# A hybrid encoder trunk in Bass: four sums of W2 quarters made by accumulating DMAs instead of GpSimd subtractions

## The chip, the cores and the metric

The kernel runs on one core of a Trainium2 chip. The metric is the device time of one execution in microseconds (us); lower is better. Engines are called by the names of the profile: PE (TensorE), PEld (its weight loads), DVE (VectorE), ACT (ScalarE), POOL (GpSimd) and SP (SyncE, which only issues DMAs here).

## The reference, cut to what matters

Two layers over 512 tokens of width 1024 in float32. Layer 0 mixes tokens by differential attention, layer 1 by a pooling mixer. Each layer then adds an MLP with a hidden width of 4096:

```
def sqrelu_mlp(h, w1, w2):
    return jnp.square(jax.nn.relu(h @ w1)) @ w2
...
h = rmsnorm(x, norm_mlp[i])
x = x + sqrelu_mlp(h, mlp_w1[i], mlp_w2[i]).astype(x.dtype)
```

The change touches only `u @ w2`, where `u` is the squared hidden activation.

## The kernel before

**Stages.** The attention layer's work fills the span up to about 310 us; then come the MLP of layer 0, the pooling mixer (about 650 to 720 us) and the MLP of layer 1. Every float32 matmul is made of three: a value is split into a part `_hi` (an ACT copy with rounding to fp32r) and a rest `_lo` (a DVE subtraction of two SBUF tensors), and PE computes hi*hi, hi*lo and lo*hi (`three`).

**MLP blocks.** The hidden width is cut into 8 blocks of 512 for each layer: b = 0 to 7 in layer 0 and 8 to 15 in layer 1. `up(b)` is 96 matmuls (`h @ w1`), then `products(b)` is 84 matmuls (`u @ w2` of the block). The last block of a layer (7 and 15, `plain`) multiplies in the ordinary way. The other 14 use a Strassen-Winograd scheme: u and W2 are each cut into four quarters, and seven products take the place of eight. For this, W2's quarters B11, B12, B21 and B22 (512 KB each) are loaded by SP, and four combinations are formed from them by POOL in `w2_sum`:

```
T1 = B12 - B11    T3 = B22 - B12 (written over B12)
T2 = B22 - T1     T4 = T2 - B21
```

The four combinations of u (S3, S1, S2, S4) are formed by DVE in `part_sum`. The products run in the order P1, P7, P6, P5, P2, P3, P4 and need B11, T3, T2, T1, B21, B22 and T4 in this order; each has 12 matmuls.

**What sets the order.** Each engine runs a written-out list and waits on semaphores. For POOL: T1, T3, T2, T4 of block b as soon as the products of block b-1 have freed T1's buffer (P5) and T4's (P4) and the quarters have landed; in blocks 1 to 4, `band(b-1)` (small masks for the pooling mixer) follows. For ACT in `up_phase(b)`: the hi part of T3, a piece of the next block's W1, the hi part of T2, another piece of W1, then the squares of the hidden tiles. For DVE in `up_phase(b)`: two lo parts of W1 (`w1_lo(b, 2)`, `(b, 3)`), lo of B11, T3, T1, one of W1, lo of T2, one of W1, and then `hidden(b, 0)`, the first look at up's output. The lo part of a matrix is written over its raw buffer, so DVE's `w2_low` for T1 also waits until T2 (which reads T1) is made, and that for T2 waits until T4 is made. In `down_phase(b)` DVE alternates lo parts with `gather`, which adds each finished product into an accumulator and frees its PSUM bank; P4 needs the lo part of T4 and the bank that P5's gather frees. Near the end of the layer `sums` combines the seven accumulators.

In block 0, POOL makes T1 between `norm_sums(0)` and `norm_root(0)`, and T3, T2, T4 after `norm_root(0)`. In block 8 it makes all four between `norm_root(1)` and `norm_sums(2)`, in the pooling stage. SP's list places `load_w2(b+1)` between the two halves of a W1 load; the load of a quarter waits for the product that last read its buffer (`PIECE_FREED`).

Of the kernel before, what the change touches and what calls it, by code (L numbers as in the profile page):

```python
# [144 lines left out]
HI_HOME = {B11: 0, B21: 0, T3: 1, B22: 1, T2: 2, T4: 2, T1: 3}  # L145
PLAIN_HOME = {B11: 0, B12: 1, B21: 2, B22: 3}
PIECES = (B11, B12, B21, B22)
PIECE_FREED = {B11: P1, B12: P7, B21: P2, B22: P3}
T_ORDER = (T1, T3, T2, T4)
U_ORDER = (A11, S3, S2, S1, A12, S4, A22)  # L150
S_ORDER = (S3, S1, S2, S4)

# [9 lines left out]
def first(b):  # L162
    return b % NB == 0
# [6 lines left out]
def before_block(b, each, last):  # L170

    layer, j = divmod(b, NB)
    return layer * ((NB - 1) * each + last) + j * each


def y_at(b):
    return before_block(b, 2 * NP, NU)
# [11 lines left out]
    return before_block(b, len(S_ORDER), 0)  # L189


def t_at(b):
    return before_block(b, len(T_ORDER), 0)


def build_trunk(nc, x, positions, norm_mix, norm_mlp, w_qkv, w_o, q_gain, k_gain, lam_q1, lam_k1,
                lam_q2, lam_k2, sub_gain, pool_w, pool_scale, w1, w2, out):
    ctx = ExitStack()
    with ctx:
# [29 lines left out]
        def sem(name):  # L229
            return ctx.enter_context(nc.semaphore(name))  # L230
# [161 lines left out]
        y_ready = sem("y_ready")  # L392
        y_added = sem("y_added")
        w2_loaded = {n: sem(f"w2_loaded_{n}") for n in PIECES}
        t_done = sem("t_done")
        w2_hi_done = sem("w2_hi_done")
        w2_lo_done = sem("w2_lo_done")
        up_piece = sem("up_piece")
# [88 lines left out]
        @block.sync  # L487
        def _(sp):
            xv = x.rearrange("a (t p) d -> p (a t) d", p=P)
            for t in range(NT):  # L490
                sp.dma_start(x_nat[:, t, :], xv[:, t, :]).then_inc(x_loaded[t], 16)
                sp.dma_start(raw[t][:].rearrange("p (a b) -> p a b", a=2), piece(0, t)).then_inc(raw_loaded[t], 16)

            def load(slab, k, src, width=PIECE):

                sp.wait_ge(w_lo_done, slab * 4 + (k - 3))
                dst = raw[k][:, 0:width]
                if len(src.shape) == 3:
                    dst = dst.rearrange("p (a b) -> p a b", a=src.shape[1])
                sp.dma_start(dst, src).then_inc(raw_loaded[k], 16)  # L500

            for s in range(1, MLP0):
                for k in range(4):
                    load(s, k, piece(s, k))

            wait_used(sp, WO0 - 1)
            for t in range(NT):
                sp.dma_start(x_again[:, t, :], xv[:, t, :]).then_inc(x_again_loaded[t], 16)

            def load_w1(b, ks):  # L510
                for k in ks:
                    load(w1_slab(b), k, w1_piece(b, k))

            def load_pool(ks):
                for k in ks:
                    load(POOLS, k, piece(POOLS, k), 2 * GW)

            def load_w2(b):
                for n in PIECES:
                    if b == 0:  # L520
                        sp.wait_ge(wo_ready, 2 * NC)
                    elif first(b):
                        sp.wait_ge(y_ready, y_at(b))
                    else:
                        sp.wait_ge(y_ready, y_at(b - 1) + 2 * PIECE_FREED[n] + 2)
                    sp.dma_start(w2_raw[n][:], w2_piece(b, n)).then_inc(w2_loaded[n], 16)

            load_w1(0, range(4))
            load_w1(1, range(4))
            load_w2(0)  # L530
            for b in range(2 * NB - 1):
                if b == NB - 2:
                    load_pool((0, 1))
                    load_w2(b + 1)
# [12 lines left out]

            ov = out.rearrange("a (t p) d -> p (a t) d", p=P)
            for n, (t, nh) in enumerate(UNITS):
                sp.wait_ge(y_added, y_at(2 * NB - 1) + n + 1)  # L550
                sp.dma_start(ov[:, t, nh * BANK:(nh + 1) * BANK], sum_part((t, nh))).then_inc(stored[n % 4], 16)
            for k in range(4):
                sp.wait_ge(stored[k], 16 * (NU // 4))
# [3 lines left out]
        def _(pool):  # L557
# [174 lines left out]

            def w2_sum(b, n):

                if n == T1:
                    pool.wait_ge(w2_loaded[B11], 16 * (b + 1))
                    pool.wait_ge(w2_loaded[B12], 16 * (b + 1))
                    if not first(b):
                        pool.wait_ge(y_ready, y_at(b - 1) + 2 * P5 + 2)
                    one, two = B12, B11  # L740
                elif n == T3:
                    pool.wait_ge(w2_loaded[B22], 16 * (b + 1))
                    pool.wait_ge(t_done, t_at(b) + 1)
                    one, two = B22, B12
                elif n == T2:
                    one, two = B22, T1
                else:
                    pool.wait_ge(w2_loaded[B21], 16 * (b + 1))
                    pool.wait_ge(t_done, t_at(b) + 3)
                    if not first(b):  # L750
                        pool.wait_ge(y_ready, y_at(b - 1) + 2 * P4 + 2)
                    one, two = T2, B21
                g.tensor_tensor(w2_raw[n][:], w2_raw[one][:], w2_raw[two][:], ALU.subtract).then_inc(t_done, 1)  # L753

            def band(gi):
                w = WINDOWS[gi]
# [49 lines left out]
        def _(act):  # L806
# [24 lines left out]
            def w2_hi(b, n):  # L831

                if n in PIECES:
                    act.wait_ge(w2_loaded[n], 16 * (b + 1))
                else:
                    act.wait_ge(t_done, t_at(b) + T_ORDER.index(n) + 1)
                if plain(b):
                    home = PLAIN_HOME[n]
                    act.wait_ge(y_ready, y_at(b - 1) + 2 * (P2, P3, P4, P5)[home] + 2)
                else:  # L840
                    home = HI_HOME[n]
                    if n in (B21, B22, T4):
                        act.wait_ge(y_ready, y_at(b) + 2 * (P1, P7, P6)[home] + 2)
                    elif not first(b):
                        act.wait_ge(y_ready, y_at(b - 1) + 2 * (P2, P3, P4, P5)[home] + 2)
                a.activation(b_hi[home][:], w2_raw[n][:], ACT.Copy).then_inc(w2_hi_done, 1)  # L846
# [241 lines left out]
        def _(dve):  # L1088
# [39 lines left out]
            def w2_low(b, n):  # L1128

                if plain(b):  # L1130
                    home, order = PLAIN_HOME[n], PLAIN_ORDER
                else:
                    home, order = HI_HOME[n], W2_ORDER
                    if n != T3:
                        dve.wait_ge(t_done, t_at(b) + {B11: 1, T1: 3, T2: 4, B21: 4, B22: 3, T4: 4}[n])
                dve.wait_ge(w2_hi_done, w2_at(b) + order.index(n) + 1)
                v.tensor_tensor(w2_lo[n][:], w2_raw[n][:], f32(b_hi[home][:]), ALU.subtract).then_inc(w2_lo_done, 1)  # L1137

# [188 lines left out]
            def part_sum(b, n):  # L1327

                done = s_at(b) + S_ORDER.index(n)
                if n == S3:  # L1330
                    dve.wait_ge(u_done, CH * b + 2)
                    one, two, op = A11, "A21", ALU.subtract
                elif n == S1:
                    dve.wait_ge(u_done, CH * b + CH)
                    one, two, op = "A21", A22, ALU.add
                elif n == S2:
                    dve.wait_ge(s_done, done)
                    one, two, op = S1, A11, ALU.subtract
                else:
                    dve.wait_ge(s_done, done)  # L1340
                    one, two, op = A12, S2, ALU.subtract
                v.tensor_tensor(u_part[n], u_part[one], u_part[two], op).then_inc(s_done, 1)  # L1342

            def part_lo(b, n):
                dve.wait_ge(u_hi_done, u_at(b) + U_ORDER.index(n) + 1)
# [77 lines left out]

            def sums(b):

                def combine_sums(dst, one, two, op=ALU.add):
                    return v.tensor_tensor(acc[dst][:], acc[one][:], acc[two][:], op)

                dve.wait_ge(y_added, y_at(b))
                link(combine_sums(P2, P1, P2))  # L1430
                link(combine_sums(P6, P1, P6))
                link(combine_sums(P7, P6, P7))
                yield
                link(combine_sums(P4, P7, P4, ALU.subtract))
# [567 lines left out]
```

## Time and profile before

| | |
|---|---|
| median of 3 runs | 1052.71 us (1051.85 to 1053.17) |
| the profiled execution, its own time | 1052.46 us |
| its span, first to last instruction | 1050.7 us |
| busy share of the span | PE 94%, PEld 76%, DVE 83%, ACT 46%, POOL 41% |
| mean granted TensorE clock | 0.985 |
| read and written | 92.74 MB, mean 88 GB/s |

A busy time is the sum of an engine's recorded instructions. Matmuls are pipelined and their records overlap, so PE's stalls are read from the distances between the starts of its matmuls, not from its share. All loads of W2 quarters are one group of 64 DMAs of 512 KB each.

### The profile page before, as it was taken

What the parts mean: (1) busy time and instruction counts of PE and PEld (TensorE: products, weight loads), DVE (VectorE), ACT (ScalarE), POOL (GpSimd) and SP (SyncE); (2) the same over time, 40 slices, a digit from 0 to 9 for tenths busy, and PEclk for the clock granted to TensorE, in tenths of its full rate; (3) what the DMA queues carried; (4) which work ended last, traced back from release to release, by engine and by line L of the source; (5) the groups of instructions that cost most, each with busy time, mean ns of one, the idle gap of its engine ahead of it and who ended that gap; (6) DMA issues with size and microseconds to landing.
All of it is one profiled execution on the core that took longest, in us unless ns stands there. A gap on an engine that the chain in (4) does not pass through costs nothing.

```text
span 1050.7 us, 12852 instructions
## 1 busy us (share of the span) xinstructions
PE 989.1 (94%) x4676; PEld 802.4 (76%) x4676; DVE 874.3 (83%) x1125; ACT 479.6 (46%) x735; POOL 429.0 (41%) x377
## 2 busy tenths in 40 slices
PE   6999998889899799999999999798999999999998
PEld 5877776667677588887887887696887888788887
DVE  5667889877946999999998897676988989989884
ACT  4525555677644534425435353364452442543420
POOL 5852678556447173473840300371403304124000
PEclk9999999999999999999999999989999999999999
DMA  6423211120232333332333233301323333233102
GB/s 240 146 42 100 61 41 58 63 81 1 62 99 80 100 100 102 99 106 95 108 93 107 74 106 115 120 2 42 119 87 113 100 101 103 98 100 100 61 20 80
DMA packets 52046, 92.74 MB, mean 88 GB/s; under 512 B 8848, under 2 KB 9872, under 8 KB 51984
## 3 DMA queue, kind: packets, MB, share of 16 engines
q1 hardware_dynamic: 45888, 91.24, 27.4%
q10 hardware_dynamic: 6096, 0.69, 0.5%
q8 instruction: 37, 0.61, 0.2%
q14 instruction: 25, 0.20, 0.1%
HBM read 89.82 MB, written 2.10 MB: 87 GB/s over the span
## 4 chain that ended last, share of the span: by engine, by line
PE 53%; DVE 27%; issue 8%; POOL 5%; ACT 4%; DMA 1%; ACTq 1%; DVEq 0%; SPq 0%; POOLq 0%
PE bank L1572 51%; DVE s_s_raw L1342 3%; DVE s_acc L1360 3%; DVE s_lbB_lo L1137 3%; ACT s_u_raw L994 2%; DVE s_w_lo L1117 2%; DVE s_nmax L1227 2%; DVE s_u_raw L1324 2%; POOL s_nsum L727 2%; PE bank L1630 1%; DVE s_u_lo L1348 1%; DVE s_lt_lo L1137 1%; DVE s_p L1249 1%; DVE s_a_lo L1348 1%; POOL s_o_r L702 1%
## 5 line engine op out<-in xcount | busy, mean ns | idle before, releaser
L1572 PE MATMUL bank<-s_hT_hi,s_w_hi 128*128 128x512 f32 x512 | 200.5, 392 | 0.0
L1572 PE MATMUL bank<-s_hT_hi,s_w_lo 128*128 128x512 f32 x512 | 199.4, 389 | 0.0
L1572 PE MATMUL bank<-s_hT_lo,s_w_hi 128*128 128x512 f32 x512 | 199.4, 389 | 0.0
L1117 DVE TENSOR_TENSOR s_w_lo<-s_raw,s_w_hi 128x1024 fp32r<-128x1024 f32 x96 | 165.9, 1744 | 14.3 <-ACT s_w_hi L816 7.9
L1572 PE MATMUL bank<-s_b_hi,s_u_hi 128*128 128x512 f32 x288 | 117.1, 407 | 14.2 <-DVE s_a_lo L1348 10.4
L753 POOL TENSOR_TENSOR s_lt<-s_lbB,s_lbB 128x1024 f32<-128x1024 f32 x14 | 35.0, 2498 | 222.9 <-PE bank L1572 222.9
L846 ACT ACTIVATE s_b_hi<-s_lbB 128x1024 fp32r<-128x1024 f32 x64 | 67.3, 1054 | 128.2 <-POOL s_lbB L753 84.5
L1572 PEld LDWEIGHTS bank<-s_hT_lo,s_w_hi 128*128 128x128 f32 x512 | 96.2, 188 | 20.2 <-issue 0.5
L1572 PEld LDWEIGHTS bank<-s_hT_hi,s_w_hi 128*128 128x128 f32 x512 | 96.2, 188 | 20.2 <-issue 0.5
L1572 PEld LDWEIGHTS bank<-s_hT_hi,s_w_lo 128*128 128x128 f32 x512 | 96.1, 188 | 20.0
L1360 DVE TENSOR_TENSOR s_acc<-s_acc,bank 128x512 f32<-128x512 f32 x168 | 107.5, 677 | 2.0 <-PE bank L1572 2.0
L1137 DVE TENSOR_TENSOR s_lbB_lo<-s_lbB,s_b_hi 128x1024 fp32r<-128x1024 f32 x64 | 104.2, 1652 | 0.0
L994 ACT ACTIVATE s_u_raw<-s_u_raw 128x512 f32<-128x512 f32 x64 | 39.9, 632 | 121.2 <-DVE s_u_raw L1324 121.1
L824 ACT ACTIVATE s_w_hi<-s_raw 128x1024 fp32r<-128x1024 f32 x60 | 61.6, 1051 | 71.2 <-PE bank L1572 63.1
L1572 PE MATMUL bank<-s_lbB_lo,s_u_hi 128*128 128x512 f32 x232 | 91.5, 394 | 0.0
L1572 PE MATMUL bank<-s_w_hi,s_hT_hi 128*128 128x512 f32 x192 | 80.1, 417 | 8.4 <-DVE s_val L1191 3.8
L1572 PE MATMUL bank<-s_b_hi,s_s_lo 128*128 128x512 f32 x224 | 87.2, 389 | 0.0
L1572 PEld LDWEIGHTS bank<-s_b_hi,s_u_hi 128*128 128x128 f32 x288 | 54.8, 190 | 35.5 <-issue 20.8
L1572 PE MATMUL bank<-s_w_hi,s_hT_lo 128*128 128x512 f32 x192 | 77.1, 402 | 0.0
L1572 PE MATMUL bank<-s_w_lo,s_hT_hi 128*128 128x512 f32 x192 | 76.9, 401 | 0.0
L1572 PE MATMUL bank<-s_b_hi,s_u_lo 128*128 128x512 f32 x176 | 68.8, 391 | 0.0
L1572 PE MATMUL bank<-s_b_hi,s_s_hi 128*128 128x512 f32 x168 | 65.5, 390 | 1.0 <-DVE s_s_lo L1348 1.0
(195 smaller groups left out, 2186.8 us busy)
## 6 DMA issues: line engine op xcount, KB each, us to landing
s_raw<-in_mlp_w SPq DMA_DIRECT2D x64, 512.0 KB, 3.8
s_lbB<-in_mlp_w SPq DMA_DIRECT2D x64, 512.0 KB, 3.3
s_raw<-in_attn_w_qkv SPq DMA_DIRECT2D x24, 512.0 KB, 4.2
s_raw<-in_attn_w_o SPq DMA_DIRECT2D x8, 512.0 KB, 3.4
s_x_nat<-in_x SPq DMA_DIRECT2D x4, 512.0 KB, 8.5
s_x_again<-in_x SPq DMA_DIRECT2D x4, 512.0 KB, 5.2
out<-s_acc SPq DMA_DIRECT2D x8, 256.0 KB, 2.0
s_raw<-in_pool_w SPq DMA_DIRECT2D x4, 256.0 KB, 2.6
```

Source lines behind the costliest of these rows:

```text
L727: g.tensor_tensor(nsum[:], first_sum, nsq[:, c % 2, :], ALU.add).then_inc(n_summed, 1)
L753: g.tensor_tensor(w2_raw[n][:], w2_raw[one][:], w2_raw[two][:], ALU.subtract).then_inc(t_done, 1)
L824: a.activation(w_hi[0][:, k * PIECE:(k + 1) * PIECE], raw[k][:], ACT.Copy).then_inc(w_hi_done, 1)
L846: a.activation(b_hi[home][:], w2_raw[n][:], ACT.Copy).then_inc(w2_hi_done, 1)
L994: a.activation(u_raw[:, f, :], u_raw[:, f, :], ACT.Square).then_inc(u_done, 1)
L1117: v.tensor_tensor(w_lo[slot][:, cols], raw[k][:], f32(w_hi[slot][:, cols]), ALU.subtract)\
L1137: v.tensor_tensor(w2_lo[n][:], w2_raw[n][:], f32(b_hi[home][:]), ALU.subtract).then_inc(w2_lo_done, 1)
L1227: last = v.tensor_reduce(nmax[:, i % 2, m:m + 1], bank[2 * (i % 2) + m][:], AX.X, ALU.max, negate=True)
L1324: v.scalar_tensor_tensor(u_raw[:, f, :], up_bank(b, f)[:], 0.0, r_bc[:], ALU.max, ALU.mult)\
L1342: v.tensor_tensor(u_part[n], u_part[one], u_part[two], op).then_inc(s_done, 1)
L1360: last = v.tensor_tensor(dst, dst, src, ALU.add)
L1572: return nc.tensor.matmul(o, lhsT, rhs, start=start, stop=stop, **kw)
```

## The change

POOL's four subtractions in each of the 14 blocks become four DMAs that POOL issues (`g.dma_start(..., accum_op=ALU.add)`): the DMA reads its source, adds it to what its destination holds, and writes the sum there. Since these DMAs only add, all combinations become sums (T1 = B11 + B12, T3 = B12 + B22, T2 = B22 + T1, T4 = B21 + T2). The signs are moved into the combinations of the activations (`part_sum`) and of the accumulators (`sums`); two instructions in each block and two in `sums` become `scalar_tensor_tensor`, where one operand is negated.

An accumulating DMA needs one term in its destination first. So SP also loads B11 into T1's buffer, B22 into T2's and B21 into T4's: seven loads in a block instead of four. T1 and T3 add a quarter straight from HBM; T2 and T4 add T1 and T2 from SBUF. SP's loads wait for the products in the order in which these free the buffers (`FREED_BY`). Each T has its own semaphore. The lo part of B11, B21, B22 and T4 no longer waits for a T; that of T1 still waits for T2 and that of T2 for T4.

```
-PIECE_FREED = {B11: P1, B12: P7, B21: P2, B22: P3}
+FREED_BY = {B11: P1, B12: P7, T2: P6, T1: P5, B21: P2, B22: P3, T4: P4}
+LOAD_ORDER = tuple(FREED_BY)
+T_PARTS = {T1: (B11, B12), T3: (B12, B22), T2: (B22, T1), T4: (B21, T2)}
...
+def sums_to(b):
+    return before_block(b, 1, 0) + 1
...
             def load_w2(b):
-                for n in PIECES:
+                for n in PIECES if plain(b) else LOAD_ORDER:
...
-                        sp.wait_ge(y_ready, y_at(b - 1) + 2 * PIECE_FREED[n] + 2)
-                    sp.dma_start(w2_raw[n][:], w2_piece(b, n)).then_inc(w2_loaded[n], 16)
+                        sp.wait_ge(y_ready, y_at(b - 1) + 2 * FREED_BY[n] + 2)
+                    if n in PIECES:
+                        sp.dma_start(w2_raw[n][:], w2_piece(b, n)).then_inc(w2_loaded[n], 16)
+                    else:
+                        sp.dma_start(w2_raw[n][:], w2_piece(b, T_PARTS[n][0])).then_inc(t_loaded[n], 16)
...
             def w2_sum(b, n):
...
-                g.tensor_tensor(w2_raw[n][:], w2_raw[one][:], w2_raw[two][:], ALU.subtract).then_inc(t_done, 1)
+                if n == T3:
+                    pool.wait_ge(w2_loaded[B12], 16 * (b + 1))
+                else:
+                    pool.wait_ge(t_loaded[n], 16 * sums_to(b))
+                two = T_PARTS[n][1]
+                if two in PIECES:
+                    src = w2_piece(b, two)
+                else:
+                    pool.wait_ge(t_done[two], 16 * sums_to(b))
+                    src = w2_raw[two][:]
+                g.dma_start(w2_raw[n][:], src, accum_op=ALU.add).then_inc(t_done[n], 16)
...
-                    if n != T3:
-                        dve.wait_ge(t_done, t_at(b) + {B11: 1, T1: 3, T2: 4, B21: 4, B22: 3, T4: 4}[n])
+                    if n in (T1, T2):
+                        dve.wait_ge(t_done[T2 if n == T1 else T4], 16 * sums_to(b))
...
-                v.tensor_tensor(u_part[n], u_part[one], u_part[two], op).then_inc(s_done, 1)
+                if n in (S1, S3):
+                    last = v.tensor_tensor(u_part[n], u_part[one], u_part[two], ALU.subtract)
+                else:
+                    last = v.scalar_tensor_tensor(u_part[n], u_part[one], -1.0, u_part[two], ALU.mult, ALU.subtract)
+                last.then_inc(s_done, 1)
```

## Rows read from the trace of the kernel before

**Rows 1.** The page, busy time and share of the span of each engine.

```profile
PE 989.1 (94%) x4676; PEld 802.4 (76%) x4676; DVE 874.3 (83%) x1125; ACT 479.6 (46%) x735; POOL 429.0 (41%) x377
```

**Rows 2.** Windows, products of block 2: PE, PEld, DVE, ACT, POOL, clock, DMA share, GB/s.

```profile
434.04:453.58 19.54, 19.39 (x84) 15.77 (x85) 19.27 (x27) 10.82 (x14) 2.39 (x1) 1.00 0.33 108
```

**Rows 3.** Timeline of PE, block 2: start us, us, then [idle before].

```profile
434.04 0.47 PE L1572 MATMUL bank<-s_b_hi,s_u_hi 128*128 128x512 f32 x1 [0.43 <-DVE s_a_lo L1348]
...
450.24 0.39 PE L1572 MATMUL bank<-s_b_hi,s_s_lo 128*128 128x512 f32 x1
450.77 0.47 PE L1572 MATMUL bank<-s_b_hi,s_u_hi 128*128 128x512 f32 x1
...
453.58 0.39 PE L1572 MATMUL bank<-s_hT_hi,s_w_hi 128*128 128x512 f32 x1
```

**Rows 4.** Timeline of DVE, end of block 2 and start of block 3.

```profile
445.72 2.58 DVE L1348 TENSOR_TENSOR s_u_lo<-s_u_raw,s_u_hi 128x512 fp32r<-128x512 f32 x1
...
454.73 6.02 DVE L1117 TENSOR_TENSOR s_w_lo<-s_raw,s_w_hi 128x1024 fp32r<-128x1024 f32 x2
...
469.66 1.21 DVE L1117 TENSOR_TENSOR s_w_lo<-s_raw,s_w_hi 128x1024 fp32r<-128x1024 f32 x1
471.46 0.69 DVE L1324 SCALAR_TENSOR_TENSOR s_u_raw<-bank,s_r_bc 128x512 f32<-128x512 f32 x1 [0.59 <-PE bank L1572]
```

**Rows 5.** Timeline of POOL, the sums T1 and T3 for block 3.

```profile
445.36 2.39 POOL L753 TENSOR_TENSOR s_lt<-s_lbB,s_lbB 128x1024 f32<-128x1024 f32 x1 [11.86 <-PE bank L1572]
453.94 2.40 POOL L753 TENSOR_TENSOR s_lbB<-s_lbB,s_lbB 128x1024 f32<-128x1024 f32 x1 [6.20 <-DMA s_lbB<-in_mlp_w]
```

**Rows 6.** The tile s_u_lo on DVE, blocks 1 and 14: ns min/median/max, first and last start.

```profile
L1348 DVE TENSOR_TENSOR s_u_lo<-s_u_raw,s_u_hi x2: 687/1652/2617, 399.7 to 403.8; 128x512 fp32r<-128x512 f32 x2
...
L1348 DVE TENSOR_TENSOR s_u_lo<-s_u_raw,s_u_hi x2: 683/684/685, 988.4 to 992.5; 128x512 fp32r<-128x512 f32 x2
```

**Rows 7.** Timeline of PE before P4, blocks 0 and 13.

```profile
366.34 0.39 PE L1572 MATMUL bank<-s_b_hi,s_s_lo 128*128 128x512 f32 x1
367.17 0.47 PE L1572 MATMUL bank<-s_b_hi,s_u_hi 128*128 128x512 f32 x1 [0.45 <-DVE s_acc L1357]
...
955.38 0.39 PE L1572 MATMUL bank<-s_b_hi,s_s_lo 128*128 128x512 f32 x1
955.91 0.47 PE L1572 MATMUL bank<-s_b_hi,s_u_hi 128*128 128x512 f32 x1
```

**Rows 8.** W2 loads (L526): all 64, then first and last of four issued together.

```profile
DMA to landing us min/median/max: 3.1/3.3/7.4
...
L526 SPq DMA_DIRECT2D s_lbB<-in_mlp_w x1: 368/368/368, 318.0 to 318.0; - x1
DMA to landing us min/median/max: 3.5/3.5/3.5
...
L526 SPq DMA_DIRECT2D s_lbB<-in_mlp_w x1: 467/467/467, 319.4 to 319.4; - x1
DMA to landing us min/median/max: 7.1/7.1/7.1
```

**Rows 9.** Timelines of POOL, DVE and PE, start of block 0.

```profile
334.52 2.38 POOL L753 TENSOR_TENSOR s_lbB<-s_lbB,s_lbB 128x1024 f32<-128x1024 f32 x1
336.86 2.83 POOL L753 TENSOR_TENSOR s_lt<-s_lbB,s_lt 128x1024 f32<-128x1024 f32 x1
...
344.04 1.27 DVE L1324 SCALAR_TENSOR_TENSOR s_u_raw<-bank,s_r_bc 128x512 f32<-128x512 f32 x2
...
347.51 0.77 PE L1572 MATMUL bank<-s_b_hi,s_u_hi 128*128 128x512 f32 x1 [4.78 <-DVE s_a_lo L1348]
```

**Rows 10.** Timelines, pooling stage: POOL's T4 for block 8, DVE and PE beside it.

```profile
692.08 2.40 POOL L753 TENSOR_TENSOR s_lt<-s_lt,s_lbB 128x1024 f32<-128x1024 f32 x1
...
693.16 1.86 DVE L1300 SCALAR_TENSOR_TENSOR s_hT_lo<-s_xT,s_gcol,s_hT_hi 128x512 fp32r<-128x512 f32 x1 [1.52 <-ACT s_hT_hi L979]
...
696.64 0.33 PE L1572 MATMUL bank<-s_band_hi,s_zn_hi 128*128 128x136 f32 x1 [0.69 <-DVE s_zn_lo L1521]
```

More of the change, by code:

```diff
@@ L189, in s_at @@
     return before_block(b, len(S_ORDER), 0)
-def t_at(b):
-    return before_block(b, len(T_ORDER), 0)
+def sums_to(b):
+    return before_block(b, 1, 0) + 1
 def build_trunk(nc, x, positions, norm_mix, norm_mlp, w_qkv, w_o, q_gain, k_gain, lam_q1, lam_k1,
@@ L394, in build_trunk @@
         w2_loaded = {n: sem(f"w2_loaded_{n}") for n in PIECES}
-        t_done = sem("t_done")
+        t_loaded = {n: sem(f"t_loaded_{n}") for n in (T1, T2, T4)}
+        t_done = {n: sem(f"t_done_{n}") for n in T_ORDER}
         w2_hi_done = sem("w2_hi_done")
@@ L733, in w2_sum @@
             def w2_sum(b, n):
-                if n == T1:
-                    pool.wait_ge(w2_loaded[B11], 16 * (b + 1))
+                if n == T3:
                     pool.wait_ge(w2_loaded[B12], 16 * (b + 1))
[L738 to L746, printed above, removed]
-                else:
[L748 to L752, printed above, removed]
-                g.tensor_tensor(w2_raw[n][:], w2_raw[one][:], w2_raw[two][:], ALU.subtract).then_inc(t_done, 1)
+                else:
+                    pool.wait_ge(t_loaded[n], 16 * sums_to(b))
[6 more added lines that the diff above has]
+                g.dma_start(w2_raw[n][:], src, accum_op=ALU.add).then_inc(t_done[n], 16)
             def band(gi):
@@ L835, in w2_hi @@
                 else:
-                    act.wait_ge(t_done, t_at(b) + T_ORDER.index(n) + 1)
+                    act.wait_ge(t_done[n], 16 * sums_to(b))
                 if plain(b):
@@ L1331, in part_sum @@
                     dve.wait_ge(u_done, CH * b + 2)
-                    one, two, op = A11, "A21", ALU.subtract
+                    one, two = A11, "A21"
                 elif n == S1:
                     dve.wait_ge(u_done, CH * b + CH)
-                    one, two, op = "A21", A22, ALU.add
+                    one, two = A22, "A21"
                 elif n == S2:
                     dve.wait_ge(s_done, done)
-                    one, two, op = S1, A11, ALU.subtract
+                    one, two = S1, A11
                 else:
                     dve.wait_ge(s_done, done)
-                    one, two, op = A12, S2, ALU.subtract
-                v.tensor_tensor(u_part[n], u_part[one], u_part[two], op).then_inc(s_done, 1)
+                    one, two = A12, S2
+                if n in (S1, S3):
[3 more added lines that the diff above has]
+                last.then_inc(s_done, 1)
             def part_lo(b, n):
@@ L1424, in sums, with less_sums @@
             def sums(b):
+                def less_sums(dst, one, two):
+                    return v.scalar_tensor_tensor(acc[dst][:], acc[one][:], -1.0, acc[two][:], ALU.mult, ALU.subtract)
                 def combine_sums(dst, one, two, op=ALU.add):
@@ L1433, in sums @@
                 yield
-                link(combine_sums(P4, P7, P4, ALU.subtract))
+                link(combine_sums(P4, P7, P4))
                 yield
-                link(combine_sums(P1, P7, P5))
+                link(less_sums(P1, P7, P5))
                 yield
-                link(combine_sums(P3, P3, P5))
-                link(combine_sums(P3, P3, P6))
+                link(less_sums(P3, P3, P5))
+                link(combine_sums(P3, P3, P6, ALU.subtract))
                 yield
```

## The prediction

> **What bounds the kernel now.** I read the page first, then PE's timeline across one MLP block, then DVE's and POOL's beside it, and last the loads. PE is busy 94% of the span, DVE 83%, POOL 41% [rows 1]. So POOL's time is worth nothing in itself; what counts is what its subtractions do to PE through another engine or a wait.
>
> The products of block 2 run from 434.04 to 453.58, at full clock and with DVE busy 19.27 of 19.54 us [rows 2]. Between 434.04 and 450.24 PE starts 72 matmuls, 0.228 us apart on average [rows 3]. At that pace the block's 180 matmuls take 41.0 us, with the stops below about 41.8. Two places lose time: a stop of 0.43 us before P1, which waits for DVE's a_lo, and one before P4: 450.24 to 450.77 is 0.53 us instead of 0.23, and P4's 12 matmuls then take 2.81 us instead of 2.73 [rows 3]. So P4's stop costs 0.38 us.
>
> P4's stop comes from POOL. At 445.36 it starts T1 of the next block, 2.39 us long [rows 5]. DVE starts the lo part of A22 at 445.72 and is at it for 2.58 us [rows 4]. This instruction takes 0.68 us where nothing is beside it. The lo part of T4 and P5's gather stand behind it in DVE's list, and P4 needs both. The trace has its own control. Each block has two such lo parts (of A12 and A22): in block 1 the longer one took 2617 ns; in block 14, behind which there is no T1 to make, neither took more than 685 ns [rows 6], and PE has no such stop there. A second collision: POOL's T3 at 453.94 [rows 5] and the T2 and T4 that follow lie beside two lo parts of W1 that take 6.02 us together [rows 4], where one alone takes 1.21. It costs nothing now: DVE still waits 0.59 us for PE before `hidden(0)` at 471.46 [rows 4].
>
> **The change part by part, and the sum.**
>
> *The subtractions go* (56 of POOL's instructions). P4's stop goes in blocks 1 to 5 and 9 to 13 (0.38 us, in one of them 0.53), 4.0 us in ten blocks; the last of them is 955.38 to 955.91. In block 0 it is 366.34 to 367.17, 0.83 instead of 0.23, with 0.08 for the restart: 0.7 us [rows 7]. Sum: 4.7 us, from which nothing is taken back as long as no other wait is later than P4. P4 waits for DVE alone here, and DVE comes 2.58 - 0.68 = 1.9 us earlier to a stop of 0.3 us. In the pooling stage T4 of block 8 (692.08) lies beside DVE's lo part at 693.16, 1.86 us instead of 0.75, and PE waits 0.69 us for what comes next on DVE [rows 10]: 0.7 us more. The stops before P1 stay.
>
> *An accumulating DMA: its price.* No row shows one. The nearest is a load of the same 512 KB: 3.3 us from issue to landing, at least 3.1 [rows 8]; that is the lower bound. Four such loads issued within 1.4 us landed 3.5 us after the first issue (321.5) and 7.1 us after the last (326.5) [rows 8]. So three more loads took 5.0 us, 1.7 us each, and this is what one costs the DMA engines; the other 1.6 us are latency. A sum reads its destination as well as its source. I double the 1.7 and keep the latency: 5.0 us. The upper bound is the longest landing in this group, 7.4 us [rows 8]. I take 5.0, since the doubling is the only difference that the change's text shows.
>
> The Trainium skill, "Collectives: The Full Stack", section "The bandwidth ceiling: the fold count and why AG ≠ RS ≠ AR", says that adding in a DMA costs no time of its own, but halves the rate because two sources are read, with 31 GB/s for a DMA engine as its figure for plain copies. No run here shows it yet. By that the moving takes an estimated 2.1 us instead of my 3.4, and a sum about 3.7 us with the same latency.
>
> *The chain of DMAs, steady blocks.* T1's base load can be issued when P5 is done (445.2, as POOL's T1 starts at 445.36 [rows 5]) and lands at 448.5. Then T1, T2 and T4 follow one another, each waiting for the one before: 15 us, 463.5; T3 shares the queue between T1 and T2 and may add up to 1 to 2 us: 465. The deadline: `hidden(0)` starts at 471.46, and the lo parts of T2 and of W1 must come before it, 1.1 us each (469.66 to 471.46 holds the last and the 0.59 of idle time) [rows 4]; so T4 must have landed by 469.2. That leaves 4 to 5 us: hidden, cost 0. The cover is gone when one DMA takes over (469.2 - 448.5)/3 = 6.9 us. Above that, each microsecond costs 3 us in a block, in 12 blocks (1 to 6 and 9 to 14; block 8's are made far ahead).
>
> *More traffic.* A block now moves 8 quarters, 33% of the DMA engines' time [rows 2]. Three more loads and four sums at double price make 19 at 1.7 us, 32 of 41.8 us or 77%. SP's list only gets waits that come in the order of the products, and the W1 loads behind them wait for DVE's lo parts of the following block anyway. Hidden, 0.
>
> *Block 0.* Here nothing covers the sums. POOL makes T3 at 334.52 and T2 until 339.69 [rows 9]; ACT's hi parts and the second W1 lo part follow, `hidden(0)` starts at 344.04 and PE has been idle 4.78 us when P1 starts at 347.51 [rows 9]. Now T3 is issued at 334.5 and lands at 339.5; T2 is right behind it in the queue and lands one service later, 342.9. That is 3.2 us later than 339.7, and it goes straight to PE. As a formula, for a DMA of A us: late by 2A - 6.8 us (issue at 334.5, A for T3, A - 1.6 of service for T2, against 339.7). Bounds: A of 3.3 gives nothing, A of 7.4 gives 8.0 us. I take 3.2. T4 lands at about 348, before DVE reaches the lo part of T2.
>
> *Block 8.* POOL now waits for T1 before it issues T2, and for T2 before T4, with `norm_sums(2)` behind. Counting back three sums of 2.4 us from T4 at 692.08 [rows 10], T1 starts at about 684.8. Two DMAs of 5.0 us later, at 694.8, T4 can be issued, and before, T4 ended at 694.5. Cost 0 up to there, and about 1 us for each further microsecond of a DMA.
>
> *The signs.* Two `scalar_tensor_tensor` in place of `tensor_tensor` in a block, of 512 columns each, and two in `sums` of each layer: DVE's instruction of that kind in the same stage takes 0.69 us [rows 4], about as much. 0.
>
> Sum: -4.7 - 0.7 + 3.2 = -2.2 us. The profiled execution took 1052.46 us, 0.25 below the median of 1052.71, so the forecast for the median is 1050.5 us.
>
> **The rivals.**
>
> *The chain is too slow (slower).* Place: T4's landing against DVE's lo part of T2 in each steady block. It decides from 6.9 us per DMA. At the 7.4 of [rows 8] each of 12 blocks loses 3 x 7.4 - 20.7 = 1.5 us, 18 us, and block 0 loses 8: 1052.7 + 18 + 8 - 5.4 = 1073 us. For it speaks that T3, the bases and the W1 loads share the engines in just these 20 us; against it the 4 us of slack.
>
> *The start of block 0 eats the gain (same).* The steady blocks behave as forecast, but T2 of block 0 lands later. It decides from a DMA of about 5.5 us; at 5.9 it is 2 x 5.9 - 6.8 = 5.0 us late: 1052.7 + 5.0 - 5.4 = 1052.3 us. For it speaks that the doubling is only my estimate.
>
> *The sums are as fast as a load (faster by more).* At the lower bound of 3.3 us T2 of block 0 lands at 339.5 and costs nothing: 1052.7 - 5.4 = 1047.3 us. For it speaks that the load's 1.7 us of service are at the pace of reads from HBM, and T2 and T4 read SBUF alone. By the rate that the Trainium skill's "Collectives: The Full Stack" gives (3.7 us, in the section named above) block 0 would lose an estimated 0.6 us, for 1047.9 us.
>
> *P4's stop stays (slower).* It would if POOL's writing of descriptors held DVE up as the subtraction did: 1052.7 - 0.7 + 3.2 = 1055.2 us, near no change if block 0 loses less. The trace has no DMA issued by POOL, so it can't be excluded.
>
> The Trainium skill, "SBUF — State Buffer", section "Who interferes with whom", says that only two-port modes of DVE block descriptor writing on GpSimd, and that a DVE instruction with two SBUF inputs is held up by GpSimd reading SBUF alone. The 2617 ns of [rows 6] agree with the second half; by the first this rival falls.
>
> **How the numbers follow.** Chances: as forecast 0.30; chain too slow 0.27; sums as fast as a load 0.22; block 0 eats the gain 0.14; P4's stop stays 0.07. The forecast is the likeliest, 1050.5 us, and its own range is 1047.3 to 1053. To hold 8 in 10, the range must take in more than half of the slow chain: up to 1073, its price at 7.4 us. That leaves 0.13 above, and 0.04 below 1047. 0.2% of the time is 2.1 us, about what a measurement of this kernel can tell from no change. The forecast lies at this edge (1050.6), so 0.18 of its 0.30 counts as faster and 0.12 as the same. Faster is 0.18 + 0.22 = 0.40. Same is 0.12, with 0.12 of the eaten gain and 0.02 of the stop that stays: 0.26. Slower is the rest of these two and the slow chain: 0.34.
>
> **What the changed profile would show.** Right: DVE's s_u_lo at 0.68 us in all blocks, PE's starts before P4 0.23 apart, the period from P1 to P1 0.4 us shorter, near 41.4 us, DMAs by POOL landing in 4 to 6 us, and PE's wait before P1 of block 0 grown from 4.8 to about 8 us. Wrong: DVE idle before the lo part of T1 or T2, released by a DMA, `hidden(0)` late in every block, and a period above 42 us; then the chain was too slow. A P4 stop that is still there with short s_u_lo would mean that I named the wrong cause.

## The result, and the profile after

The kernel after takes 1117.6 us (median of 4 runs, 1110.7 to 1121.2) against 1052.9 us for the kernel before beside it. The ratio is 1.059, with an interval of 1.053 to 1.066. That is 65 us slower, 67 above the forecast and 45 above the top of the range.

First, the page of the kernel after: busy time, the DMA queues, the chain of work that ended last, two groups of costly instructions, and DMA issues with their median landing.

```profile
PE 1010.9 (91%) x4676; PEld 820.7 (74%) x4676; DVE 780.7 (70%) x1125; ACT 481.7 (43%) x735; POOL 323.9 (29%) x377
...
q1 hardware_dynamic: 57312, 113.26, 30.6%
q0 software_dynamic: 11648, 29.36, 15.2%
...
PE 39%; DMA 22%; DVE 18%; issue 11%; POOL 6%; ACT 3%; ACTq 0%; POOLq 0%; SPq 0%; DVEq 0%
...
L1578 PE MATMUL bank<-s_b_hi,s_u_hi 128*128 128x512 f32 x288 | 128.0, 444 | 56.9 <-DVE s_a_lo L1351 55.3
...
L1136 DVE TENSOR_TENSOR s_lt_lo<-s_lt,s_b_hi 128x1024 fp32r<-128x1024 f32 x42 | 51.3, 1222 | 46.5 <-DMA s_lt<-s_lt 46.2
...
s_lt<-s_lt POOLq DMA_DIRECT2D x28, 512.0 KB, 7.3
s_lt<-in_mlp_w POOLq DMA_DIRECT2D x14, 512.0 KB, 6.0
s_lbB<-in_mlp_w POOLq DMA_DIRECT2D x14, 512.0 KB, 8.9
```

What the change was to take away is gone: DVE is busy 781 us instead of 874, POOL 324 instead of 429 [rows 1]. In their place stands a chain. A fifth of the time is a DMA that something waits for, DVE waits 46 us for the DMAs of T2 and T4, and PE waits 55 us for `a_lo` before P1.

POOL's timeline in the same stage as [rows 5], the sums for block 3 (start us, us, then the idle time before and what ended it):

```profile
462.93 1.26 POOL L752 DMA_DIRECT2D s_lt<-in_mlp_w  x1 [17.52 <-DMA s_lt<-in_mlp_w]
469.00 1.23 POOL L752 DMA_DIRECT2D s_lbB<-in_mlp_w  x1 [4.81 <-DMA s_lt<-in_mlp_w]
469.73 1.43 POOL L752 DMA_DIRECT2D s_lt<-s_lt  x1
481.67 0.86 POOL L752 DMA_DIRECT2D s_lt<-s_lt  x1 [10.51 <-DMA s_lt<-s_lt]
```

T1 is issued at 462.93, T3 at 469.00, T2 at 469.73, T4 at 481.67. From issue to landing T1 takes 5.8 us, T3 9.0, T2 11.2 (until 481.0) and T4 5.3 (until 487.0); these four together, by the line of the code that issues them:

```profile
DMA to landing us min/median/max: 5.3/7.4/11.2
```

The second line of the timeline is the one to stop at: in the code, T3 waits only for B12's load, issued at 453.73, and yet it goes out when T1 has landed, 6.07 us after T1.

DVE's timeline of the same stage, against [rows 4], and PE's at the stop behind it, before P1 of block 3, to hold against P1 of block 2 in [rows 3]:

```profile
479.16 1.22 DVE L1136 TENSOR_TENSOR s_lbB_lo<-s_lbB,s_b_hi 128x1024 fp32r<-128x1024 f32 x1 [7.73 <-ACT s_b_hi L845]
...
487.01 1.23 DVE L1136 TENSOR_TENSOR s_lt_lo<-s_lt,s_b_hi 128x1024 fp32r<-128x1024 f32 x1 [3.66 <-DMA s_lt<-s_lt]
488.15 1.22 DVE L1116 TENSOR_TENSOR s_w_lo<-s_raw,s_w_hi 128x1024 fp32r<-128x1024 f32 x1
489.29 1.28 DVE L1323 SCALAR_TENSOR_TENSOR s_u_raw<-bank,s_r_bc 128x512 f32<-128x512 f32 x2
```

```profile
488.67 0.39 PE L1578 MATMUL bank<-s_hT_hi,s_w_lo 128*128 128x512 f32 x1
493.26 0.77 PE L1578 MATMUL bank<-s_b_hi,s_u_hi 128*128 128x512 f32 x1 [4.21 <-DVE s_a_lo L1351]
493.82 0.63 PE L1578 MATMUL bank<-s_lbB_lo,s_u_hi 128*128 128x512 f32 x1
494.25 0.63 PE L1578 MATMUL bank<-s_b_hi,s_a_lo 128*128 128x512 f32 x1
...
498.09 0.63 PE L1578 MATMUL bank<-s_b_hi,s_a_lo 128*128 128x512 f32 x1
498.52 0.63 PE L1578 MATMUL bank<-s_b_hi,s_u_hi 128*128 128x512 f32 x1
498.94 0.45 PE L1578 MATMUL bank<-s_lbB_lo,s_u_hi 128*128 128x512 f32 x1
```

T4 lands, DVE's lo part of T2 starts at 487.01 with it, `hidden(0)` follows at 489.29 and P1 at 493.26. PE has stood for 4.2 us, and then the starts of P1's matmuls are 0.43 us apart instead of 0.23. Windows of both kernels over the same 200 us, before first (columns as in [rows 2]):

```profile
400.00:600.00 200.00, 197.86 (x864) 161.27 (x863) 187.23 (x188) 80.65 (x100) 96.02 (x112) 1.00 0.32 99
```

```profile
400.00:600.00 200.00, 183.63 (x753) 149.62 (x752) 135.34 (x174) 75.85 (x96) 51.08 (x108) 0.92 0.61 163
```

The loss has two parts, then: PE idle, 16.4 us instead of 2.1, and a granted clock of 0.92 instead of 1.00. The period from P1 to P1 (taken at P1's third matmul) was 41.67 to 41.93 us (42.4 and 44.2 in the two that begin with a layer's first block) and is now 46.1 to 48.5. Added up over twelve periods that makes 60.3 us of the 65.7 by which the profiled span grew; block 0 adds 3.2, and the rest lies ahead of it and behind the P1s of blocks 6 and 14. The idle part can be read from the page. The group of matmuls that each P1 begins with, on the page of the kernel before:

```profile
L1572 PE MATMUL bank<-s_b_hi,s_u_hi 128*128 128x512 f32 x288 | 117.1, 407 | 14.2 <-DVE s_a_lo L1348 10.4
```

PE's wait for `a_lo` grew from 10.4 to 55.3 us, and these 44.9 us are the larger part of the loss.

### The profile page after: what moved, and what is told of

Its sections match the earlier page's. It is cut to its first block, busy times and chain, and to the rows that moved or that the text cites. A ratio compares the mean times of both kernels' runs of the same rounds, so it can differ in the third digit from the quotient of the medians.

```text
span 1116.4 us, 12824 instructions
## 1 busy us (share of the span) xinstructions
PE 1010.9 (91%) x4676; PEld 820.7 (74%) x4676; DVE 780.7 (70%) x1125; ACT 481.7 (43%) x735; POOL 323.9 (29%) x377
## 3 DMA queue, kind: packets, MB, share of 16 engines
q1 hardware_dynamic: 57312, 113.26, 30.6%
q0 software_dynamic: 11648, 29.36, 15.2%
## 4 chain that ended last, share of the span: by engine, by line
PE 39%; DMA 22%; DVE 18%; issue 11%; POOL 6%; ACT 3%; ACTq 0%; POOLq 0%; SPq 0%; DVEq 0%
PE bank L1578 37%; DMA s_lt<-s_lt 18%; DMA s_lt<-in_mlp_w 4%; DVE s_w_lo L1116 3%; DVE s_lt_lo L1136 2%; ACT s_u_raw L993 2%; DVE s_nmax L1226 2%; PE bank L1636 1%; POOL s_lt L752 1%; DVE s_qkn L1178 1%; DVE s_s_raw L1342 1%; DVE s_u_raw L1323 1%; DVE s_p L1248 1%; POOL s_lbB L752 1%; DVE s_a_lo L1351 1%
## 5 line engine op out<-in xcount | busy, mean ns | idle before, releaser
L1578 PE MATMUL bank<-s_b_hi,s_u_hi 128*128 128x512 f32 x288 | 128.0, 444 | 56.9 <-DVE s_a_lo L1351 55.3
L1136 DVE TENSOR_TENSOR s_lbB_lo<-s_lbB,s_b_hi 128x1024 fp32r<-128x1024 f32 x64 | 77.6, 1221 | 97.1 <-ACT s_b_hi L845 97.0
L1363 DVE TENSOR_TENSOR s_acc<-s_acc,bank 128x512 f32<-128x512 f32 x168 | 112.3, 683 | 34.4 <-PE bank L1578 34.4
L1116 DVE TENSOR_TENSOR s_w_lo<-s_raw,s_w_hi 128x1024 fp32r<-128x1024 f32 x96 | 117.9, 1245 | 20.3 <-ACT s_w_hi L823 12.2
L1578 PEld LDWEIGHTS bank<-s_b_hi,s_u_hi 128*128 128x128 f32 x288 | 61.8, 215 | 76.9 <-issue 60.8
L1578 PE MATMUL bank<-s_lbB_lo,s_u_hi 128*128 128x512 f32 x232 | 102.6, 442 | 0.0
L752 POOL DMA_DIRECT2D s_lt<-in_mlp_w x14 | 17.5, 1253 | 273.7 <-DMA s_lt<-in_mlp_w 273.7
L845 ACT ACTIVATE s_b_hi<-s_lt 128x1024 fp32r<-128x1024 f32 x42 | 44.6, 1061 | 107.5 <-DMA s_lt<-in_mlp_w 83.3
L1136 DVE TENSOR_TENSOR s_lt_lo<-s_lt,s_b_hi 128x1024 fp32r<-128x1024 f32 x42 | 51.3, 1222 | 46.5 <-DMA s_lt<-s_lt 46.2
L752 POOL DMA_DIRECT2D s_lt<-s_lt x28 | 32.1, 1146 | 133.8 <-DMA s_lt<-s_lt 133.8
```

The costliest lines, as they stand in the source:

```text
L752: g.dma_start(w2_raw[n][:], src, accum_op=ALU.add).then_inc(t_done[n], 16)
L1116: v.tensor_tensor(w_lo[slot][:, cols], raw[k][:], f32(w_hi[slot][:, cols]), ALU.subtract)\
L1363: last = v.tensor_tensor(dst, dst, src, ALU.add)
L1578: return nc.tensor.matmul(o, lhsT, rhs, start=start, stop=stop, **kw)
```

## The experiments

Each time stands beside runs of the kernel before on the same chip, 1052.8 to 1053.9 us.

**More room for descriptors.** Descriptors are the lists that tell the DMA engines what to move. The program sets the size of the area for those of POOL's DMAs, in bytes per partition.

```
-    nc = bacc.Bacc("TRN2", target_bir_lowering=False, num_devices=1, dynamic_dma_scratch_size=1024)
+    nc = bacc.Bacc("TRN2", target_bir_lowering=False, num_devices=1, dynamic_dma_scratch_size=2048)
```

> The changed kernel with one number changed: the space for POOL's descriptors is 2048 bytes per partition instead of 1024. In the changed kernel T3's DMA is issued when T1's has landed (469.0 against 462.9), though B12, all it waits for by its text, landed long before. Theory ring: one accumulating DMA from HBM fills so much of the 1024 bytes that a second one must wait for the first; with 2048 bytes T3 is issued about 1.3 us behind T1, the last sum of a block lands 4 to 5 us earlier, and the stop of 4 us before P1 is gone or nearly so: 1050 to 1065 us. Rival engines: the 16 DMA engines (0.76 busy in this stretch) are what is short; T1 and T3 side by side only take longer each, and the time stays at 1095 to 1118 us. Rival length: three sums in a chain are too long whatever is beside them (6 to 9 us each): 1095 us or more, with T3 landing earlier but T4 not.

Measured: 1063.9 us (1062.1 to 1066.1), ratio 1.009 (1.006 to 1.012). POOL's timeline in the stage of block 2:

```profile
457.58 1.25 POOL L752 DMA_DIRECT2D s_lt<-in_mlp_w  x1 [14.39 <-DMA s_lt<-in_mlp_w]
458.36 1.72 POOL L752 DMA_DIRECT2D s_lbB<-in_mlp_w  x1
464.36 0.90 POOL L752 DMA_DIRECT2D s_lt<-s_lt  x1 [4.27 <-DMA s_lt<-in_mlp_w]
473.63 0.86 POOL L752 DMA_DIRECT2D s_lt<-s_lt  x1 [8.37 <-DMA s_lt<-s_lt]
```

T3 now follows T1 after 0.78 us, and 53.7 of the 64.6 us come back. PE's wait for `a_lo` falls from 55.3 to 24.4 us. What is left is still the chain: issue of T1 to landing of T4 lasts 21.3 us (457.6 to 478.8) instead of 24.1, and it begins 14.7 us behind P1 instead of 17.9. DVE's idle time is no measure of the loss: before the lo parts of T1, T2 and T4 it is 61.0 us here and 46.2 in the slower kernel after. What costs is a late `hidden(0)`.

**T3 ahead of T1**, with the small area kept, and then **both mends together**.

```
-T_ORDER = (T1, T3, T2, T4)
+T_ORDER = (T3, T1, T2, T4)
```

> The changed kernel with POOL's list in another order: T3, T1, T2, T4, the space for descriptors left at 1024 bytes. T3 can then be issued when B12 has landed (about 457 where T1's own first term lands at 462.9), so it is nearly done before T1 is issued, and the chain T1, T2, T4 has POOL's queue for itself: about 462.9 + 6 + 5.5 + 5.3 = 480 instead of 487. Theory place (T3 between T1 and T2 costs the 7 us): the stop before P1 goes in the steady blocks, 1048 to 1058 us. Rival length: T1, T2 and T4 alone still need more than 20.7 us from the landing of T1's first term: above 1080 us.

> The kernel after with both mends, T3 ahead of T1 on POOL and 2048 bytes of descriptor space. Chain theory: each mend alone left T1, T2 and T4 some 20 us long and 1 to 4 us late; T3 first takes T3's service out of the chain, the bigger space lets T1 be issued while T3 is under way (it already could, since T3 lands before T1's base). So about as T3 first alone or somewhat better: 1056 to 1066, still above before. Descriptor theory as the main cause: both together give all back, 1050 or less.

Measured: T3 first alone 1068.7 us (1062.0 to 1076.3), ratio 1.014 (1.008 to 1.020), above what was expected and below its rival. With both mends 1061.9 us (1056.8 to 1071.7), ratio 1.0075 (1.0039 to 1.0111). The two mends don't add up. T3 first keeps T3 out of the chain, but now it slows T1's base load (median landing 5.6 us instead of 3.4), and the chain still lasts 19.7 us, from 454.4 to 474.1 with T3 first alone. An order or a bigger area moves T3; neither makes T1, T2 and T4 short enough.

**One link less**, with 2048 bytes. T4's source is B22 from HBM, so T4 is not the sum it should be; it reads no T2, and DVE's lo of T2 waits for no T4. DMAs and bytes are as many as in the 1063.9 us run.

```
-                if two in PIECES:
+                if n == T4:
+                    src = w2_piece(b, B22)
+                elif two in PIECES:
...
-                    if n in (T1, T2):
-                        dve.wait_ge(t_done[T2 if n == T1 else T4], 16 * sums_to(b))
+                    if n == T1:
+                        dve.wait_ge(t_done[T2], 16 * sums_to(b))
```

> The kernel after with 2048 bytes of descriptor space and with T4 made as B21 plus B22 from HBM, so T4 is not the sum it should be; it no longer reads T2, waits for no sum, and DVE's lo of T2 no longer waits for T4. The number of accumulating DMAs and their bytes stay. Chain theory: with 2048 bytes 1063.9 was left because T1, T2 and T4 in a row last about 21 us (457.6 to 478.9) where the lo of T2 is due near 475; with one link less the last DMA that DVE waits for is T2, 5 to 6 us earlier, the wait of the lo goes, PE's stop before each block falls by over 1 us, and the time is 1046 to 1053. Traffic theory (what is left comes from the queue's load and slower other loads, not from the number of links): 1060 to 1065, with PE's wait for s_a_lo as in that run, 24 us in all.

Measured: 1048.5 us (1046.8 to 1050.1), ratio 0.994 (0.9915 to 0.9963). POOL's queue on its page, then DVE's timeline in the stage of block 2: lo of T1, lo of T2 and the first of `hidden(0)`.

```profile
q0 software_dynamic: 13440, 29.36, 16.2%
```

```profile
466.92 1.23 DVE L1138 TENSOR_TENSOR s_lt_lo<-s_lt,s_b_hi 128x1024 fp32r<-128x1024 f32 x1 [1.01 <-DMA s_lt<-s_lt]
...
469.20 1.22 DVE L1138 TENSOR_TENSOR s_lt_lo<-s_lt,s_b_hi 128x1024 fp32r<-128x1024 f32 x1
...
473.91 0.69 DVE L1325 SCALAR_TENSOR_TENSOR s_u_raw<-bank,s_r_bc 128x512 f32<-128x512 f32 x1 [1.99 <-PE bank L1580]
```

The expectation of the chain is met, that of the traffic isn't: the software queue's share is 16.2% of this shorter span, each sum as dear as before, and yet the period is 41.3 us. So it is not the load of the queue. Nor is it the time at which T4 arrives: T4 still lands 35.7 us after the P1 of the block before (median), where it landed after 36.4 in the 1063.9 us run. What cost was the wait that the third link brings with it. T4 reads T2's buffer, so the lo part of T2, which is written over that buffer, and `hidden(0)` behind it stood until T4 had landed. Here they don't, and DVE waits 1.99 us for PE again before `hidden(0)`.

**No accumulation**: plain copies in place of the four sums, so the sums are left out. Everything else, 1024 bytes too, is as in the kernel after.

```
-                g.dma_start(w2_raw[n][:], src, accum_op=ALU.add).then_inc(t_done[n], 16)
+                g.dma_start(w2_raw[n][:], src).then_inc(t_done[n], 16)
```

> The kernel after with the accumulation taken out of T1 to T4's DMAs (they are plain copies of the same size, between the same places and behind the same waits), so the sums are left out of the computation. Service theory: a sum costs 3.0 us of the sixteen engines against 1.6 of a load, and this is what makes the four DMAs land after 6 to 11 us; plain copies take 1.6 us, land after some 4 us, and the queue's service falls from 15 to about 8 per cent. T4 then lands two to three us per link earlier, the wait of the lo of T1 and T2 goes, and the time is 1048 to 1056. Descriptor theory (the small descriptor space alone holds T3 back until T1 has landed): T3 is still issued only when T1 lands, whatever the service; if that place is what costs, the time stays above 1070. Both can hold in part: then T3 is still held back, but for 4 us rather than 6, and the time is 1055 to 1070.

> The same kernel as the one without the accumulation (1046.6 us), for a trace at the ordinary clock, which that run's profiled execution had not. Service theory: on the four DMAs the software queue's share falls from 15.2 to about 7.5 per cent of the span (1.4 to 1.5 us for each, as a load), each lands after 4 to 6 us, T3 is still issued only when T1 lands (1024 bytes of descriptor space), and yet T4 lands before 472 on the clock of block 2, so that DVE's lo of T1 and T2 waits for no DMA.

Measured: 1046.6 us, ratio 0.991 (0.988 to 0.994), and 1046.9 us the second time, 0.993 (0.991 to 0.996). From the trace of the second: queues and median landings, then POOL's timeline.

```profile
q1 hardware_dynamic: 57312, 113.26, 32.9%
q0 software_dynamic: 8064, 29.36, 7.8%
...
s_lt<-s_lt POOLq DMA_DIRECT2D x28, 512.0 KB, 3.9
...
s_lt<-in_mlp_w POOLq DMA_DIRECT2D x14, 512.0 KB, 5.0
s_lbB<-in_mlp_w POOLq DMA_DIRECT2D x14, 512.0 KB, 5.8
```

```profile
447.89 0.78 POOL L752 DMA_DIRECT2D s_lt<-in_mlp_w  x1 [19.65 <-DMA s_lt<-in_mlp_w]
448.66 0.73 POOL L752 DMA_DIRECT2D s_lbB<-in_mlp_w  x1
453.68 0.57 POOL L752 DMA_DIRECT2D s_lt<-s_lt  x1 [4.29 <-DMA s_lt<-in_mlp_w]
461.44 0.54 POOL L752 DMA_DIRECT2D s_lt<-s_lt  x1 [7.19 <-DMA s_lt<-s_lt]
```

The service expectation is met: 7.8% of 1044.1 us over 56 DMAs is 1.45 us each, against 15.2% of 1116.4, 3.03 us each, with the sum. One point of it was missed, and it says more than a hit. T3 was expected to go on waiting for T1, since the area was still 1024 bytes; it goes out 0.77 us behind T1. So it isn't any two DMAs that don't fit into 1024 bytes. It isn't any two sums either: in the kernel after, T2 goes out at 469.73, while T3 is under way until 478.0, and so in all 14 blocks. What never goes out together there is T1 and T3, two sums that read HBM.

The packets tell them apart. The 56 DMAs are 8064 packets as copies, 144 each. As sums they are 11648, and 13440 in the run where T4 reads HBM too. These numbers come out with 272 packets for a sum that reads HBM and 144 for one that reads SBUF: 28 of each make 11648, 42 and 14 make 13440. With 1024 bytes 416 packets were under way together (T3 and T2) and 544 were not (T1 and T3); with 2048 bytes 544 were. That the longer descriptor lists fill the area is the reading that all runs fit; the filling itself stands in no trace.

This run takes away the hold and the dearer service at once, so it doesn't tell their shares; the run with 2048 bytes does that for the hold.

**The signs alone**: POOL adds in place of its subtractions, four loads as before, and the new signs in the activations and in `sums`.

```
+                g.tensor_tensor(w2_raw[n][:], w2_raw[one][:], w2_raw[two][:], ALU.add).then_inc(t_done[n], 1)
```

> The changed kernel's signs alone: the four combinations of W2 are sums, made by POOL's tensor_tensor add out of place as in the kernel before, with four loads in a block and the waits of before. The instructions of DVE with a negated operand stay. Theory: the signs cost nothing, 1051.5 to 1054 us, same within 0.2% as the kernel before. Rival: scalar_tensor_tensor in the chain to the second and third product costs 0.1 to 0.5 us in each of 14 blocks, 1054 to 1060 us.

Measured: 1052.4 us, ratio 0.999 (0.997 to 1.001). The signs cost nothing.

**POOL's T1 later**, in the kernel before: it waits for P3 instead of P5 and so no longer lies beside the lo part of A22.

```
                 if n == T1:
...
-                        pool.wait_ge(y_ready, y_at(b - 1) + 2 * P5 + 2)
+                        pool.wait_ge(y_ready, y_at(b - 1) + 2 * P3 + 2)
```

> The kernel before with one wait changed: POOL starts T1 when the sixth product (P3) of the block before is done, not the fourth (P5). T1 then runs beside DVE's gathers, which read one SBUF tensor, instead of beside the lo part of A22, which reads two. Theory: the stop before P4 is caused by T1 on POOL alone and goes, 4 to 4.7 us, and nothing else gets late: 1047.5 to 1049.5 us, and A22's lo part takes 0.68 us in all blocks. Rival: T1 five microseconds later makes T3, T2 and T4 late, or T3 and T2 slow down the lo parts of W1 so much more that the first hidden tile is late: no gain or slower, 1053 to 1060 us.

Measured: 1050.4 us (1046.7 to 1051.9, 10 runs), ratio 0.996 (0.994 to 0.998). The tile `s_u_lo` on DVE, all blocks, against [rows 6]:

```profile
L1348 DVE TENSOR_TENSOR s_u_lo<-s_u_raw,s_u_hi x28: 677/688/693, 358.1 to 986.8; 128x512 fp32r<-128x512 f32 x28
```

No lo part takes 2.6 us any more, and the period is 41.3 us. So P4's stop was T1's doing, and one product's name in one wait gets most of the gain that the change was to bring in the steady blocks: 3.1 us of 4.0.

**Two whole versions of the change.** In the first, T2 is made from HBM alone (B22, with B11 and then B12 added), with POOL's order T3, T2, T1, T2 again, T4. In the second, T4 is an add on GpSimd. Both have 2048 bytes and compute every sum.

```
+                if n == T2:
+                    g.dma_start(w2_raw[n][:], w2_piece(b, B11), accum_op=ALU.add).then_inc(t2_half, 16)
+                    return
...
+                if n == T1:
+                    pool.wait_ge(t2_half, 16 * sums_to(b))
+                    g.dma_start(w2_raw[T2][:], w2_piece(b, B12), accum_op=ALU.add).then_inc(t_done[T2], 16)
```

```
+                    g.tensor_tensor(w2_raw[T4][:], w2_raw[T2][:], w2_raw[B21][:], ALU.add).then_inc(t_done[T4], 16)
```

> A version of the change with all its sums: 2048 bytes, POOL's order T3, T2, T1, T2 again, T4, where T2 is B22 with B11 and then B12 added from HBM, and so does not read T1. A fifth accumulating DMA, 3 us more of service per block. Chain theory: the chain to T4 begins with T2's base, which is free a product earlier than T1's, and DVE's lo of T1 waits for no sum; T4 lands by about 470 on the clock of block 2, where 471 is the time at which the lo of T2 stood before; the time is 1047 to 1056. Traffic theory: the fifth sum makes every load slower, W1's and the bases, and the time is 1062 or more.

> A version with all its sums: 2048 bytes of descriptor space, T1, T3 and T2 by accumulating DMAs, and T4 by an add on GpSimd from T2 and B21, so that the last link is 1 to 2 us of GpSimd in place of a DMA of 5 to 6, and the base load of T4 goes. Chain theory: two DMA links as in the run that had two (1048.5), T4's add ends some 2 us after T2 lands, about 475, at the time where the lo of T2 stands, and the price is the slower DVE around that add: 1048 to 1054. Should the add, which also waits for the product P4 of the block before, or its readers, move DVE's lo of T1 and T2 later than a DMA would: 1055 to 1062.

Measured: T2 from HBM 1092.6 us (1087.2 to 1095.5), ratio 1.034: a miss for the chain theory as I had put it. The chain begins 13.8 us after P1 instead of 14.9 (medians, against the first run with 2048 bytes), but it lasts 25.6 us instead of 21.4. T1's and T2's DMAs now land after 9.1 us in the median, since two of them are under way nearly all the time (T3's issue is at 453.5, T2's at 456.6 and 465.4, T1's at 462.1, T4's at 475.6); PE waits 40.3 us for `a_lo`. From its page:

```profile
s_lt<-in_mlp_w POOLq DMA_DIRECT2D x42, 512.0 KB, 9.1
```

The queue's load alone doesn't stop the kernel, but it sets how long a link lasts. T4 on GpSimd: 1051.1 us (1049.2 to 1055.6, 10 runs), ratio 0.997 (0.995 to 0.999), as expected, and just faster than before. The add takes 3.33 us at 469.02, where T4's DMA took 5.3 and came later.

## Why the prediction was wrong

- **The subtractions go: right.** The stop before P4 is gone in every block, and all `s_u_lo` take 0.68 to 0.69 us. Late T1 alone gives about 0.4 us a block. The kernel without the accumulation is 6 to 7 us faster than before, where I had counted 5.4.
- **The price of a sum: the service right, the landing too low.** I doubled 1.7 us to 3.4; measured are 3.03 us against 1.58 for a load by queue share (30.6% of 1116.4 us, divided by the 216 times that 512 KB go into 113.26 MB). The rule of the Trainium skill that I weighed ("Collectives: The Full Stack", section "The bandwidth ceiling: the fold count and why AG ≠ RS ≠ AR"), half the rate for an adding DMA, agrees: 3.03 us is 2.1 times the copy's 1.45. The time I had estimated from its figure, 2.1 us, was too short. But the landing I built on my 3.4, 5.0 us, holds only for a sum from SBUF that is alone (T4); the median over all 56 was 6.9, and the largest 11.9.
- **The chain of DMAs: the step that failed.** I wrote that T3 "shares the queue between T1 and T2 and may add up to 1 to 2 us", and put T4's landing at 465 against a deadline of 469.2. Counted from T1's issue, the chain was forecast at 16.5 us and took 24.1. T1 took 5.8 us. After 1.0 us, in which T3 went out first, T2 followed and, with T3 ahead of it in the queue instead of beside T1, lasted 11.2. After 0.7 more T4 took 5.3. Of these 7.6 us too many, T2 beside T3 makes 6.2, where the term for T3 had 1 to 2; the issues behind a landing, 1.7 us, had no term, and T1 and T4 make the rest. The sign that I had named for this came true: a period above 42 us, with DVE waiting for a DMA before the lo part of T2. Mending T3's issue gave back 53.7 of the 64.6 us, and taking the last link away 15.4 more. Plain copies, with all links and 1024 bytes, gave back 70.7 by themselves, since they end 6.1 below the kernel before. The rival "the chain is too slow" named the place and the sign, but not the size: it priced the links at 7.4 us and added only idle time.
- **What the rival lacked: the clock.** P1's stop before was 0.43 us [rows 3] and the clock stayed at full. After stops of 2.6 to 4.7 us, up to thirteen matmuls start 0.43 us apart; the granted clock over the 19.54 us from P1's start is 0.85, against 1.00 in [rows 2]. That is half the clock for 5.9 us, the time of these matmuls, so they ran at its lower level, 1.2 GHz:

```profile
493.26:512.80 19.54, 19.54 (x74) 15.95 (x75) 17.36 (x26) 10.08 (x13) 3.11 (x6) 0.85 0.42 135
```

  The trace after holds 134 such starts in the products of blocks 0 to 14, that of before 11, all of them in blocks 0 and 8 behind stops of 4.8 and 2.7 us. 123 times 0.2 us is 25 us, some two fifths of the loss. The run with 2048 bytes, where the steady blocks' stops are 0.4 to 2.3 us, has 17, and 15 of these in blocks 0 and 8. Together the parts come near the whole: 44.9 us of waiting for `a_lo` and 25 of slow starts, less 5.4 for the stops that went, are 64.5 of the 65.7 us. The slow clock also feeds itself. These matmuls lie ahead of P5, which frees T1's buffer, so the next chain begins 3 us later: T1 was issued 17.9 us after P1's start (445.07), where the forecast had 14.5 (448.5 after 434.04).
- **More traffic: partly right.** The DMA share is 0.61 over blocks 2 to 5, where I had counted 0.77 of a shorter block. The run with two links shows that this load alone costs nothing, the one with a fifth sum that it stretches every link.
- **Block 0: the sum right, by luck.** PE's wait before P1 grew from 4.78 us [rows 9] to 7.97, the 3.2 us forecast:

```profile
351.03 0.77 PE L1578 MATMUL bank<-s_b_hi,s_u_hi 128*128 128x512 f32 x1 [7.97 <-DVE s_a_lo L1351]
```

  But T3 was issued at 336.02, not 334.5, and T2 landed at 344.4, not 342.9. That it cost no more means some 1.5 us of slack between T2's landing and P1 that I had not counted: two errors that cancel.
- **Block 8: the cost right, its working wrong.** T1 was issued right behind `norm_root(1)` (722.79), the place where it stood before: as forecast. But the two DMAs to T4's issue took 15.1 us instead of 10 (737.90), and `norm_sums(2)` behind them began 5 us late. At the 1 us per microsecond that I gave, this would be 5 us. From the matmul behind `norm_sums(1)` to P1 of block 8, before first:

```profile
681.57:729.55 47.98, 43.01 (x243) 37.89 (x243) 30.94 (x46) 24.67 (x43) 23.02 (x13) 0.93 0.08 22
```

```profile
719.63:765.82 46.19, 41.92 (x242) 36.90 (x243) 30.46 (x46) 24.47 (x43) 17.68 (x13) 0.94 0.38 85
```

  It takes 1.8 us less, not 5 more, and PE is idle 0.7 us less, as forecast for the stop of [rows 10]. `norm_sums(2)` had slack: its last sum ended at 710.1, 7.5 us before PE's matmul that reads it, and now it ends 3.2 us before it.
- **The signs: right**, 0 as measured alone.

## What to carry to other kernels

Count the links of a chain of DMAs, each at its landing time among the others in flight, and not at that of a lone transfer: four accumulating DMAs of 512 KB, one or two of them in flight at a time, took 5 to 11 us each. Look at what a link makes others wait for, too: what the last one cost here was the wait of the instruction that overwrites its source, not its own arrival. Look at when each one is issued as well: an issue that followed a landing for which its text doesn't wait was held here by the room for descriptors. Where an engine's work disturbs another, first try to move it in time; here one wait, moved by two products, gave as much (1050.4 us) as the best whole rewrite (1051.1). And price a new stop of PE with what the clock takes behind it: 1.4 to 3.0 us behind each of P1's stops of 2.6 us or more in the kernel after.

## What the runs showed of the hardware

An accumulating DMA of 512 KB takes the sixteen engines 3.03 us and a copy of it by the same queue 1.45. With 1024 bytes of descriptor area two copies were in flight together, and a sum from HBM with one from SBUF, but two sums from HBM were not; with 2048 bytes they were. A sum from HBM made 272 packets, a sum from SBUF and a copy 144. GpSimd's issue of a sum, 0.9 to 1.5 us in the kernel after, did not slow DVE: the 128x1024 lo parts beside one took 1.22 to 1.23 us, as elsewhere. No `s_u_lo` lay beside one there; in the run with T2 from HBM thirteen did and took 0.68 to 0.69. The Trainium skill, "SBUF — State Buffer", section "Who interferes with whom", infers that `tensor_tensor` on DVE does not hold up the writing of descriptors, as it takes only the read side of the port pair that it shares with GpSimd. The traces agree for the other direction, DVE's own time.
